# Attention: two heads' narrow pieces are scored side by side as one piece

## The reference

```python
z = jnp.einsum('bqhd,bkhd->bhqk', qi, k).astype(F32) * scale + bias_f      # scale = 64 ** -0.5, one bias a head
mask = (k_pos[None, :] < pi[:, None])[None, None]
log_keep = jnp.where(mask, jax.nn.log_sigmoid(-z), 0.0)
tail = lax.cumsum(log_keep, axis=3, reverse=True)
tail_excl = jnp.concatenate([tail[..., 1:], jnp.zeros_like(tail[..., :1])], axis=-1)
w = jnp.where(mask, jnp.exp(jax.nn.log_sigmoid(z) + tail_excl), 0.0)
return jnp.einsum('bhqk,bkhd->bqhd', w, v)
```

## Time and profile before

| | |
|---|---|
| median of 3 runs | 1952.86 us (1952.48 to 1954.66) |
| the profiled execution, its own time | 1951.84 us |
| its span in the trace | 1950.1 us |
| PE busy over the span | 1834.9 us (94%) |
| DVE busy | 1045.7 us (54%) |
| ACT busy | 862.4 us (44%) |
| attention, first to last sigmoid | 1414.67 to 1839.76 us |

### The profile page before, as it was taken

The page is one execution under the profiler, slowest core; times in us unless marked ns, Lnnn a source line. Parts: engine busy times, 40 slices in busy tenths (PEclk is TensorE's granted clock), DMA queues, the critical chain, the costliest instruction groups (busy, mean ns, idle before and its releaser), DMA issues. The chain is left out here.

```text
span 1950.1 us, 29623 instructions
## 1 busy us (share of the span) xinstructions
PE 1834.9 (94%) x10871; PEld 1482.5 (76%) x10871; DVE 1045.7 (54%) x1909; ACT 862.4 (44%) x1844; POOL 80.9 (4%) x140
## 2 busy tenths in 40 slices
PE   5899999999999999699989999999899998888998
PEld 2688888888888888577778767888777776666577
DVE  4553535353534344434446345754278888888852
ACT  3743323232433232423335223433277778888720
POOL 2000000000000000000000001011000000000000
PEclk8899999999999999899999999999889999999999
DMA  9221213040403122463424653222332326534152
GB/s 314 81 90 56 90 55 113 31 144 0 144 22 122 46 98 89 134 218 98 129 62 166 202 203 102 84 90 95 94 78 76 82 68 190 174 120 130 39 173 92
DMA packets 185054, 214.21 MB, mean 110 GB/s; under 512 B 45688, under 2 KB 143426, under 8 KB 183921
## 3 DMA queue, kind: packets, MB, share of 16 engines
q1 hardware_dynamic: 171226, 165.67, 27.9%
q0 software_dynamic: 13728, 47.21, 6.3%
HBM read 164.10 MB, written 48.76 MB: 109 GB/s over the span
## 5 line engine op out<-in xcount | busy, mean ns | idle before, releaser
L460 PE MATMUL rt_acc<-rt_w_hi,rt_h_hi 128*128 128x512 f32 x512 | 207.5, 405 | 7.4 <-DVE rt_w_lo L1004 6.5
L462 PE MATMUL rt_acc<-rt_w_hi,rt_h_lo 128*128 128x512 f32 x512 | 201.2, 393 | 0.0
L461 PE MATMUL rt_acc<-rt_w_lo,rt_h_hi 128*128 128x512 f32 x512 | 200.6, 392 | 0.0
L943 DVE TENSOR_TENSOR rt_by_cos<-rt_raw,rt_cos 128x256 f32<-128x256 f32 (+1 forms) x72 | 30.6, 424 | 282.1 <-ACT rt_raw L784 282.1
L2638 PE MATMUL kq_acc<-kq_w_hi,kq_h 128*128 128x512 f32 x384 | 153.5, 400 | 4.8 <-DVE kq_w_lo L2460 4.8
L2639 PE MATMUL kq_acc<-kq_w_lo,kq_h 128*128 128x512 f32 x384 | 150.2, 391 | 0.0
L2641 PE MATMUL kq_acc<-kq_w_hi,kq_h 128*128 128x512 f32 x384 | 150.2, 391 | 0.0
L460 PE MATMUL rt_acc_g<-rt_g_hi,rt_h_hi 128*128 128x256 f32 x512 | 149.2, 291 | 0.0
L795 ACT COPY rt_qk_t<-rt_tr 128x256 f32<-128x256 f32 (+1 forms) x72 | 26.1, 363 | 275.5 <-PE rt_tr L648 275.5
L461 PE MATMUL rt_acc_g<-rt_g_lo,rt_h_hi 128*128 128x256 f32 x512 | 144.6, 283 | 0.0
L462 PE MATMUL rt_acc_g<-rt_g_hi,rt_h_lo 128*128 128x256 f32 x512 | 144.6, 282 | 0.0
(11 more groups left out here) (365 smaller groups left out, 4172.4 us busy)
## 6 DMA issues: line engine op xcount, KB each, us to landing
ro_a_raw<-retained SPq DMA_DIRECT2D x16, 1024.0 KB, 6.0
op_ada<-in_ada_w SPq DMA_DIRECT2D x8, 1024.0 KB, 12.8
rt_w_raw<-in_ret_w_in SPq DMA_DIRECT2D x16, 512.0 KB, 5.0
rt_w_raw<-in_ret_w_in SPq DMA_DIRECT2D x8, 1024.0 KB, 7.7
rt_old<-in_state_ret SPq DMA_DIRECT2D x8, 1024.0 KB, 6.0
rt_g_raw<-in_ret_w_in SPq DMA_DIRECT2D x8, 1024.0 KB, 5.4
out_st_sample<-rt_new POOLq DMA_DIRECT2D x8, 1024.0 KB, 7.9
kq_w_raw<-in_sb_w_in SPq DMA_DIRECT2D x4, 2048.0 KB, 8.9
```

The source lines that it names most:

```text
L460: nc.tensor.matmul(dst, h_hi[:, k, cols], w_hi[:, k, :], start=k == 0, stop=False)
L461: nc.tensor.matmul(dst, h_hi[:, k, cols], w_lo[:, k, :], start=False, stop=False)
L462: last = nc.tensor.matmul(dst, h_lo[:, k, cols], w_hi[:, k, :], start=False, stop=k == KD - 1)
```

## The change

Where a span has 256 columns or fewer, its two heads become one piece: two scores side by side in one `z` bank (256 or 512 columns in all), one pair of sigmoids, two scans, one product, one set of transposes, one copy, one `attend`. Since one sigmoid instruction can add only one bias a row, TensorE adds the biases of joined pieces: a matmul of a [64, 128] matrix of 1/32 (`share`) with a column of `bias_parts`, read with step 0 over the piece's columns, between the `q_hi` and the `q_lo` products; the sigmoids of joined pieces have no bias operand. There are 32 joined pieces (units 0, 1, 4 and 5 of each pair), 96 of 512 and 32 of 384 columns, and 8 of the samples: 168. The samples come every 9 pieces or more instead of every 11, the gates' slices come in periods of 8 pieces instead of 10, and the slots of the keys move: for a pair that follows a falling one they now lie at the start of the falling pair (its tiles 7 and 6), and both heads' first halves are turned before the second halves. `y` becomes a part of `g_out`.

```diff
-    def __init__(self, u, hh, c0, n, first, last, b=None):
-        self.u, self.hh, self.c0, self.n, self.first, self.last, self.b = u, hh, c0, n, first, last, b
+    def __init__(self, u, heads, c0, n, first, last, b=None):
+        self.u, self.heads, self.c0, self.n, self.first, self.last, self.b = u, heads, c0, n, first, last, b
+        self.scans = max(1, len(heads))
+        self.wide = n * self.scans
+        self.closes = heads[-1:] != (0,)
...
-                for hh in range(2):
-                    pieces.append(Piece(u, hh, c0, cols, n == 0, n == len(spans) - 1))
+                for heads in [(0, 1)] if cols <= NB // 2 else [(0,), (1,)]:
+                    pieces.append(Piece(u, heads, c0, cols, n == 0, n == len(spans) - 1))
         HALF = len(pieces) // 2
-        S_FIRST, S_EVERY = HALF + 16, 11
+        S_FIRST, S_EVERY = HALF + 15, 9
         for b in range(DB):
-            pieces.insert(S_FIRST + S_EVERY * b, Piece(None, None, 0, sa.NK, False, False, b))
+            at = S_FIRST + S_EVERY * b
+            while not pieces[at - 1].closes:
+                at += 1
+            pieces.insert(at, Piece(None, (), 0, sa.NK, False, False, b))
...
+        bias_parts = sb("bias_parts", [P // 2, AH], F32R)
+        share = sb("share", [P // 2, P], F32R)
...
-        y = sb("y", [P, 4, NS])
+        y = g_out[:, 0, NB // 2:NB].rearrange("p (d c) -> p d c", d=4)
...
-        START, FIRST_SLOT, PERIOD, FILL = KD, 3, 30, 24
+        START, FIRST_SLOT, PERIOD, FILL = KD, 3, 24, 19
...
-            split_at = begins[pair * NPT - 5] if rising else begins[pair * NPT - 6] + 1
+            split_at = begins[pair * NPT - 5] if rising else begins[pair * NPT - 8] + 2
             for hh in range(2):
                 k_split_slots[split_at + hh] = 2 * pair + hh
-            for n, p in enumerate(free_slots(begins[pair * NPT - (4 if rising else 5)], 4)):
-                k_slots[p] = (2 * pair + n // 2, n % 2)
+            for n, p in enumerate(free_slots(begins[pair * NPT - 4] if rising else begins[pair * NPT - 7] + 1, 4)):
+                k_slots[p] = (2 * pair + n % 2, n // 2)
             assert p < begins[pair * NPT] - 1
-        new_slots = {p: n for n, p in enumerate(free_slots(HALF - 6, 3))}
+        new_slots = {p: n for n, p in enumerate(free_slots(HALF - 9, 3))}
...
-                    pe.wait_ge(k_taken, 2 * (2 * pair + at.hh + 1))
+                    pe.wait_ge(k_taken, 4 * (pair + 1) if pair else 2)
+                if at.first and at.u == NPT // 2:
+                    pe.wait_ge(k_taken, 4)
                 if at.first:
                     pe.wait_ge(q_lo_s, g + 1)
                 own = c0 + n == (t + 1) * P
-                dst, keys = z[:, p % 2, 0:n], k_t[:, pair % 2, at.hh, c0:c0 + n]
-                nc.tensor.matmul(dst, q_hi[:, g % 2, at.hh, at.u % QG, :], keys, start=True, stop=False)
-                last = nc.tensor.matmul(dst, q_lo[:, g % 2, at.hh, at.u % QG, :], keys, start=False, stop=not own)
-                if own:
-
-                    last = nc.tensor.matmul(dst[:, n - P:n], ident_r[:], far_r[:], start=False, stop=True)
+                for i, hh in enumerate(at.heads):
+                    dst, keys = z[:, p % 2, i * n:(i + 1) * n], k_t[:, pair % 2, hh, c0:c0 + n]
+                    nc.tensor.matmul(dst, q_hi[:, g % 2, hh, at.u % QG, :], keys, start=True, stop=False)
+                    if len(at.heads) == 2:
+                        head = 2 * pair + hh
+                        nc.tensor.matmul(dst, share[:], bias_parts[:, head:head + 1].to_broadcast([P // 2, n]), start=False, stop=False)
+                    last = nc.tensor.matmul(dst, q_lo[:, g % 2, hh, at.u % QG, :], keys, start=False, stop=not own)
+                    if own:
+                        last = nc.tensor.matmul(dst[:, n - P:n], ident_r[:], far_r[:], start=False, stop=True)
...
-                if at.hh == 0:
+                if not at.closes:
                     return
-                wait_taken(pe, p - 1)
+                if len(at.heads) == 1:
+                    wait_taken(pe, p - 1)
...
+                        if len(at.heads) == 2:
+                            weights = w_t[:, p % WR, (hh * blocks + b) * P:(hh * blocks + b + 1) * P]
+                        else:
+                            weights = w_t[:, (p - 1 + hh) % WR, b * P:(b + 1) * P]
...
+                dst, src = (keep[:, p % 2, 0:n], take[:, p % TR, 0:n]), z[:, p % 2, 0:n]
+                if len(at.heads) == 2:
+                    nc.scalar.activation(dst[0], src, ACT.Sigmoid, scale=-(DH ** -0.5))
+                    nc.scalar.activation(dst[1], src, ACT.Sigmoid, scale=DH ** -0.5).then_inc(sticks, 1)
+                    return
...
+            nc.vector.tensor_scalar(share[:], ps.ident[0:P // 2, :], 0.0, 1.0 / 32, ALU.mult, ALU.add)
+            nc.vector.tensor_scalar(bias_parts[:], bias_row[0:P // 2], DH ** 0.5, None, ALU.mult).then_inc(prepared, 1)
+            dve.wait_ge(prepared, 3)
+            low = slice(32, 64)
+            nc.vector.scalar_tensor_tensor(bias_parts[low], bias_row[low], DH ** 0.5, bias_parts[low].bitcast(F32),
+                                           ALU.mult, ALU.subtract)
...
+                    c0 = at.c0
+                    for i, hh in enumerate(at.heads):
+                        ring, k = after_key[:, hh], keep[:, p % 2, i * n:(i + 1) * n]
+                        seed = 1.0 if at.first else ring[:, c0 + n:c0 + n + 1]
+                        nc.vector.tensor_tensor_scan(ring[:, c0:c0 + n][:, ::-1], k[:, ::-1], k[:, ::-1], seed, ALU.mult,
+                                                     ALU.bypass).then_inc(scanned, 1)
+                    later = after_key[:, at.heads[0]:at.heads[-1] + 1, c0 + 1:c0 + n + 1]
+                dve.wait_ge(scanned, scans_done(p))
+                own = take[:, p % TR, 0:at.wide]
+                if len(at.heads) == 2:
+                    own = own.rearrange("p (h c) -> p h c", h=2)
+                elif at.b is None:
+                    later = later.rearrange("p h c -> p (h c)")
+                nc.vector.tensor_tensor(own, own, later, ALU.mult).then_inc(weighed, 1)
...
+                    dve.wait_ge(g_stored[0], 16 * (NPT // 2))
```

More of the change, by code:

```diff
@@ L1197, in sums_done, with scans_done, k_at @@
         def sums_done(p):
-            return len([n for n in range(p + 1) if pieces[n].b is not None or pieces[n].hh == 1])
+            return len([n for n in range(p + 1) if pieces[n].closes])
         def read_by_sums(p):
-            return sums_done(p + 1 if pieces[p].hh == 0 else p)
+            return sums_done(p if pieces[p].closes else p + 1)
+        def scans_done(p):
+            return sum(pieces[n].scans for n in range(p + 1))
+        def k_at(head, part):
+            return 4 * (head // 2) + 2 * part + head % 2
         TR, WR = 3, 4
@@ L1395, in _ @@
             v_slots = {ends[NPT * pair - 1] + 4: pair + 1 for pair in range(1, PAIRS - 1)}
-            g_slots = {ends[NPT * pair - 1] + 9: pair + 1 for pair in range(1, PAIRS - 1)}
+            g_slots = {ends[NPT * pair - 1] + 8: pair + 1 for pair in range(1, PAIRS - 1)}
             turned_at = {max(p for p in page_slots if page_slots[p][0] == b) + 1: b for b in range(DB)}
@@ L1404, in _ @@
                     load_samples()
-                if at.first and at.u % NPT == 0 and at.hh == 0 and 0 < at.u // NPT < PAIRS - 1:
+                if at.b is None and p == begins[at.u] and at.u % NPT == 0 and 0 < at.u // NPT < PAIRS - 1:
                     load_k(at.u // NPT + 1)
@@ L1480, in turn_k @@
                 last.then_inc(k_turned, 1)
-                kq_taken[0] = (k_taken, 2 * head + part + 1)
+                kq_taken[0] = (k_taken, k_at(head, part) + 1)
             def turn_new(n):
@@ L1617, in _ @@
             project(KD // 2 + 2, KD // 2 + 3)
[L1618 removed]
+            turn_k(0, 1)
             score(0)
@@ L1685, in stick @@
             def stick(p):
-                at, n = pieces[p], pieces[p].n
+                at, n = pieces[p], pieces[p].wide
                 act.wait_ge(scored, p + 1)
@@ L1694, in stick @@
                 else:
-                    head = 2 * where(at.u)[0] + at.hh
+                    head = 2 * where(at.u)[0] + at.heads[0]
                     against, towards = bias[:, 1, head:head + 1], bias[:, 0, head:head + 1]
-                nc.scalar.activation(keep[:, p % 2, 0:n], z[:, p % 2, 0:n], ACT.Sigmoid, scale=-(DH ** -0.5), bias=against)
-                nc.scalar.activation(take[:, p % TR, 0:n], z[:, p % 2, 0:n], ACT.Sigmoid, scale=DH ** -0.5, bias=towards).then_inc(sticks, 1)
+                nc.scalar.activation(dst[0], src, ACT.Sigmoid, scale=-(DH ** -0.5), bias=against)
+                nc.scalar.activation(dst[1], src, ACT.Sigmoid, scale=DH ** -0.5, bias=towards).then_inc(sticks, 1)
             def take_w(p):
@@ L1737, in open_gates @@
                     act.wait_ge(merged, 1)
-                    src, n = y[:].rearrange("p d c -> p (d c)"), 4 * NS
```

(12 more changed lines are left out.)

26 lines of the change are left out of this document (12 added, 14 removed).

## The result

The changed kernel takes 1964.51 us (median of 4 runs, 1962.22 to 1966.28) against 1952.67 of the kernel before beside it: ratio 1.006, interval 1.0042 to 1.0077. It is slower, by about 12 us, and lies outside the forecast range.

A forecast was written before the change was run, and what follows sets the result against it. No engine was taken as full (79 to 89% busy); each turn lasts as its slowest engine. Gains of 19.5 and 5 us less 12 given back and 3 for joined scores made 9.5 us: 1943 us, range 1928 to 1957.

The forecast's parts named there:

- prices the bias product: On TensorE, two matmuls added to each joined piece, 64 in all, the next start 0.12 us later: 7.7 us.
- VectorE and ScalarE: Busy time in attention: VectorE's down by about 5 us and ScalarE's by 18.
- Units 0, 1, 4 and 5: The joined pieces' units: 19.5 us gained in units 4 and 5, 5 us in units 0 and 1.
- The turns' model: Attention's loop: a turn lasts about as long as its slowest engine's work; a joined turn is TensorE's, 2.3 or 2.7 us.
- Given back: Work that hung on the 32 removed turns falls on the 136 others: 12 us lost, between 7.5 and 15.
- the long scores: A joined score holds its bank's sigmoid back longer: 0.1 us on each of 32, 3 us lost.
- The query chain: Units 0 and 1: query turn, ScalarE's copy, VectorE's `q_lo` take 3.6 us, so TensorE waits 1.3 at seven places.
- The moved keys: Key turns now lie in tiles 7 and 6, among full turns, with `kq` free: nothing by itself.
- The sum: Attention's gains less its losses: 9.5 us faster, a median time of 1943 us.
- That TensorE is the bound: Rival, 20%: TensorE bounds every turn; 7.7 us added and 8 saved give no change, 1953 us.
- The long query chain: Rival, 10%: the chain in units 0 and 1 takes 6.5 us; seven waits of 4.0 cost 28: 11 slower, 1964.
- The end of the stage: Attention's last joined piece ends about 0.5 us later than a single one of 128 columns.

The follow-up runs named there:

- the run that changes nothing else: The changed kernel with its bias products on all 128 rows instead of 64 (also called 128 rows): 1946.72 us, 0.9962 of the kernel before.
- the pair in the kernel before: The kernel before, pieces not joined, `y` in `g_out`, a zero product added in each of 64 narrow pieces: 1980.0 us on 64 rows, 1956.95 on 128.
- after: The changed kernel as first measured, its bias products on 64 rows, against the kernel before: 1964.51 us, ratio 1.006.
- the run that takes most of it away: The changed kernel with 128-row bias products, plus turns of queries of tiles 0 and 1 one piece earlier: 1941.01 us, 0.9929 of the kernel before.

## Why the prediction was wrong

The step that failed is the one that prices the bias product: "The nearest row is a score product of 256 columns, where the next one starts 0.12 us later, so 7.7 us." That row is of products with 128 rows among their like. With the height of the change it cost, by the starts at two places, 0.29 us more at 128 columns and 0.38 more at 256 (0.73 and 0.85 us for a head's score against 0.44 and 0.47), so 32 x 0.29 + 32 x 0.38 = 21 us on top of 64 x 0.11 = 7. TensorE's busy time says 30.3 in place of 4.7. And I gave bounds on one side only, 3.9 from below. That the height is the cause is shown by the run that changes nothing else, and by the pair in the kernel before. The rest by its steps:

- **What I could have read.** The earlier trace rows was the right group and I took the wrong column of it, the load's duration. The same group of loads, looked at in its place, would have told more. It is of transposes of the samples' rows, on a tile of 64 by 128 like that of `share`, right behind a score:

```profile
1618.57 0.22 PE L1533 MATMUL z<-pa_far_r,pa_ident_r 128*128 128x128 f32 x1
1618.72 0.71 PE L1489 MATMUL pa_kq<-ident,sa_new_rows 64*128 64x64 f32 x8
```

  They start 0.15 us behind the score's third product, where transposes of 128 rows start 0.06 behind it (1622.46 to 1622.52), and the last of the eight (1619.20) is again 0.15 ahead of the next 128-row product (1619.36), where among themselves they are 0.06 apart. Two times 0.09 on 64 products is 12 us more, a price of 19 for moving columns this short, and a forecast near no change. A dearer place was at the samples' value products; weight loads, with the idle time ahead of each in brackets:

```profile
1667.90 0.15 PEld L1586 LDWEIGHTS pa_acc<-sa_new_rows,pa_w_t 64*32 64x32 f32 x8 [0.41 <-issue]
1668.47 0.19 PEld L1529 LDWEIGHTS z<-pa_k_t,pa_q_hi 128*128 128x128 f32 x1 [0.41 <-issue]
1668.58 0.19 PEld L1530 LDWEIGHTS z<-pa_k_t,pa_q_lo 128*128 128x128 f32 x1
```

  Before the load of 64 rows, and again before the next one of 128, the load path idles 0.41 us for nothing the profile shows, while the next of equal height follows 0.11 behind. Here the tile's columns change as well (32 and 128), so it is not the same passage, but it would have been a bound from above: two such gaps on each of 64 products, 52 us, and a range that holds the result.
- **VectorE and ScalarE** saved 6.7 and 19.7 us of busy time (5 and 18 foreseen). Right.
- **Units 0, 1, 4 and 5** were to gain 24.5 us. With 128 rows they gain 8 x (0.47 + 0.80 + 1.44 + 0.82) = 28; after 8 x (-0.13 + 0.82 + 0.89 + 0.75) = 19. The turns' model held where its price for the product held.
- **Given back**, 12 us (7 to 15) foreseen in the wide units. With 128 rows units 3, 6 and 7 give back 8 x (0.61 + 0.84 + 0.57) = 16 us and the samples' pieces 2; 18 us, where 12 and 3 for the long scores were forecast: under-sized. After, it is 29 with unit 2 and the samples. So the dear product cost 10 us where it stands and 11 more in the turns beside it. That TensorE arrives late there, and the transposes with it, fits the copies' waits (95.1 us against 77.5 with 128 rows), but isn't shown turn by turn.
- **The query chain** was to wait 7 x 1.3 = 9 us: 5 times, 5.9 us after; 6.7 with 128 rows. The mechanism is shown by the run that takes most of it away; its size was a third too big.
- **The end of the stage** was put at 0.5 us, and is 3.4 with 128 rows and 1.5 after.
- **The moved keys**, "nothing by itself": not settled. With only tiles 4 and 5 joined, units 6 and 7 are 1.0 and 0.56 longer though unit 3 isn't, which fits key turns now standing there, but nothing isolates it. The moved slot did have a cost at another place: it needs its load sooner, 17 us when the queue's order changed.
- **The sum.** With the assumed price made true (128 rows) the stage is 10.1 us shorter, where 9.5 was forecast, and the time 1946.72, where 1943 was; the end's 3.4 us is most of the difference. The 10.1 is partly luck: 28 us gained for 24.5, and 18 given back for 15.
- **The rivals.** That TensorE is the bound (no change, by its 7.7 us) had the right engine and the same wrong price. The long query chain forecast 1964, the measured time, by another mechanism: its waits came to 5.9 us in all, 2.1 at most, where it needed 2.4 at each of seven places (its chain of 4.9 us should read 4.7, 2.3 + 2.4; nothing hangs on it). The operand with step 0, which I named as what could make the product long, is innocent: it is in the cheap 128-row product too.

## What to carry to other kernels

Price an added instruction by a row of its own shape between its future neighbours, and read the distance from start to start and the idle time ahead of its load, not its duration; where no such row exists, set a bound from above as well. A small product put among tall ones is worth padding to their height; here the shares were halved and spread over twice the rows, and the product became about four times cheaper between starts. And when slots are moved, look at what feeds them: the load's place in its queue must move too.
